# Norms between two blocks and the turning of x: a new order of passes in a 31-chunk kernel

## What is computed

```
u = rms_norm(x, norm_in_g)                 # x * rsqrt(mean(x*x) + 1e-6) * g
proj = u @ w_in                            # 1024 x 4096: pool_x, pool_z, m_x, m_z
y = concat(pool_mixer(pool_x) * silu(pool_z), mlstm_branch(m_x) * silu(m_z))
h = rms_norm(x + y @ w_out, norm_out_g)
x2 = layer_norm(h, ln_in_g_2, ln_in_b_2)
hh = x2 @ w_in_2                           # gMLP, convolution and window attention parts
out = layer_norm(ALPHA * x2 + concat(ya, yb, yc) @ w_out_2, post_ln_g_2, post_ln_b_2)
```

## Time and profile before

| | us |
|---|---|
| median of 3 runs (1269.55 to 1270.44) | 1270.35 |
| the profiled execution, whole | 1271.04 |
| its span on the core | 1269.2 |
| TensorE busy | 1214.5 |
| VectorE, GpSimd, ScalarE busy | 660.3, 466.2, 350.5 |
| mean granted TensorE clock, 1 being full | 0.986 |

### The profile page before, as it was taken

The page is one execution under the profiler, slowest core; times in us unless marked ns, Lnnn a source line. Parts: engine busy times, 40 slices in busy tenths (PEclk is TensorE's granted clock), DMA queues, the critical chain, the costliest instruction groups (busy, mean ns, idle before and its releaser), DMA issues.

```text
span 1269.2 us, 15967 instructions
## 1 busy us (share of the span) xinstructions
PE 1214.5 (96%) x5976; PEld 970.7 (76%) x5976; DVE 660.3 (52%) x1226; ACT 350.5 (28%) x710; POOL 466.2 (37%) x446
## 2 busy tenths in 40 slices
PE   4999999999999999999998998889999999999995
PEld 4778778788888878787786787768888886667784
DVE  6424274522366303167767924755696525445468
ACT  6211111100021212446565411231111143443311
POOL 1042242223454223444665644234242225443333
PEclk9999999999999999999999998999999999999998
DMA  6141121234312112200114411222111110051112
GB/s 213 43 141 42 34 74 34 100 133 132 74 34 67 59 67 89 83 23 25 55 39 141 175 34 67 83 96 67 51 36 64 59 34 34 2 191 34 34 51 116
DMA packets 72702, 92.84 MB, mean 73 GB/s; under 512 B 12721, under 2 KB 51849, under 8 KB 72114
## 3 DMA queue, kind: packets, MB, share of 16 engines
q1 hardware_dynamic: 63922, 87.62, 20.6%
q10 hardware_dynamic: 8704, 4.20, 1.2%
HBM read 74.45 MB, written 18.92 MB: 74 GB/s over the span
## 4 chain that ended last, share of the span: by engine, by line
PE 86%; DVE 6%; POOL 3%; issue 2%; ACT 1%; DMA 1%; SPq 1%; ACTq 0%; POOLq 0%; DVEq 0%
PE bank L821 21%; PE bank L823 20%; PE bank L822 20%; PE bank L1049 3%; PE bank L1066 3%; PE wide L1219 2%; PE wide L901 2%; PE bank L1200 2%; PE wide L1209 2%; PE wide L1059 2%; DVE res L1879 1%; PE bank L1009 1%; PE bank L1020 1%; POOL h L721 1%; PE bank L997 1%
## 5 line engine op out<-in xcount | busy, mean ns | idle before, releaser
L609 POOL CAST whi<-wraw 128x2048 fp32r<-128x2048 f32 x32 | 60.7, 1896 | 473.5 <-PE bank L823 371.7
L821 PE MATMUL bank<-u_hi,wlo 128*128 128x512 f32 x512 | 202.9, 396 | 4.0 <-DVE u_lo L1322 4.0
L822 PE MATMUL bank<-u_lo,whi 128*128 128x512 f32 x512 | 200.6, 392 | 0.0
L823 PE MATMUL bank<-u_hi,whi 128*128 128x512 f32 x512 | 200.5, 392 | 0.0
L611 POOL TENSOR_TENSOR wlo<-wraw,whi 128x2048 fp32r<-128x2048 f32 x33 | 156.2, 4735 | 8.0 <-ACT whi L2197 5.4
L821 PE MATMUL bank<-x_hi,wlo 128*128 128x512 f32 x320 | 128.7, 402 | 7.1 <-POOL wlo L611 4.6
L823 PE MATMUL bank<-x_hi,whi 128*128 128x512 f32 x320 | 125.4, 392 | 0.0
L822 PE MATMUL bank<-x_lo,whi 128*128 128x512 f32 x320 | 125.4, 392 | 0.0
L821 PEld LDWEIGHTS bank<-u_hi,wlo 128*128 128x128 f32 x512 | 96.9, 189 | 26.7 <-DVE u_lo L1322 4.5
L823 PEld LDWEIGHTS bank<-u_hi,whi 128*128 128x128 f32 x512 | 96.9, 189 | 20.6
L822 PEld LDWEIGHTS bank<-u_lo,whi 128*128 128x128 f32 x512 | 96.9, 189 | 20.5 <-issue 0.7
(11 more groups left out here) (318 smaller groups left out, 2416.4 us busy)
## 6 DMA issues: line engine op xcount, KB each, us to landing
wraw<-in_w_in SPq DMA_DIRECT2D x27, 1024.0 KB, 5.3
wraw<-in_w_out SPq DMA_DIRECT2D x12, 1024.0 KB, 5.1
xr<-in_x SPq DMA_DIRECT2D x8, 512.0 KB, 6.2
hst<-in_x SPq DMA_DIRECT2D x4, 1024.0 KB, 5.3
hpool<-hst SPq DMA_DIRECT2D x4, 1024.0 KB, 4.1
smz<-mzs SPq DMA_DIRECT2D x16, 256.0 KB, 2.0
wraw<-nmax ACTq DMA_DIRECT2D x32, 128.0 KB, 3.0
h<-hpool SPq DMA_DIRECT2D x4, 1024.0 KB, 6.7
```

The costliest lines, as they stand in the source:

```text
L609: g_.tensor_copy(whi[w % 2][:, :, :], wraw[:, :, :]).then_inc(s["w_hi"], 1)
L821: pe.matmul(ps, al, bh, start=(k == 0), stop=False)
L822: pe.matmul(ps, ah, bl, start=False, stop=False)
L823: return pe.matmul(ps, ah, bh, start=False, stop=(k == nk - 1))
```

## The change

**At the start.** SyncE loads x's tiles 4 to 7 right after weight chunk 0, ahead of the small gain vectors; `norm_in_g` is loaded by ScalarE's queue (`l_g`). ScalarE takes a root of ones first, so that its function table is loaded early, and takes each tile's root itself from the sum of squares (scale 1/D, bias `eps`); `var_x` is gone. TensorE waits for `norm_in_g` alone, turns it, and then turns each tile of x as it is scaled, into seven banks, with the eighth group of columns at the end. The rest of `VT` is turned after tile 3 of the product. VectorE no longer splits chunk 0; GpSimd does, in four parts (`g_part`), once four tiles are scaled, and starts chunk 1 only when all eight are. TensorE takes tile 0 of the product step by step as `u_lo` and the parts come; the second four tiles of x are turned in between the steps of tile 2.

**Between the blocks.** `norm_2` is cut in three: `tile_stats`, `tile_centre` and `tile_scale`. The scaling of tile t-1 follows the addition of tile t. GpSimd does seven of the left-half gains before it splits `W_OM + 3` (three before), and of the right half five (`GAINS`), after which `W_2` is split; VectorE does the last three. The first four groups of transposes follow step 12 of `PAIR`, and tile 0 of `W_BA` goes step by step.

```diff
-    LATE_2 = 6
+    LATE_2, GAINS = 6, 5
...
             wt(0)
-            rows = [("norm_in_g", 0), ("pool_scale", 0), ("conv_b", 0), ("mh_norm_w", 0), ("skip_w", 0)]
+            for t in range(4, NT):
+                sp_.dma_start(xr[:, t, :], x_v[:, t, :]).then_inc(l_x[t], 16)
+            rows = [("pool_scale", 0), ("conv_b", 0), ("mh_norm_w", 0), ("skip_w", 0)]
...
-            for t in range(4, NT):
-                sp_.dma_start(xr[:, t, :], x_v[:, t, :]).then_inc(l_x[t], 16)
...
+            g_.wait_ge(s["v_xn"], 4)
+            g_.wait_ge(s["w_hi"], 1)
+            for part in range(4):
+                ks = slice(2 * part, 2 * part + 2)
+                g_.tensor_tensor(wlo[0][:, ks, :], wraw[:, ks, :], whi[0][:, ks, :].bitcast(F32), ALU.subtract
+                                 ).then_inc(s["g_part" if part < 3 else "w_lo"], 1)
+            g_.wait_ge(s["v_xn"], NT)
             for w in range(1, W_MX + 2):
                 split(w)
...
             for t in range(NT):
                 gain(t, 0)
-                if t == 2:
+                if t == 6:
                     split(W_OM + 3)
-            for t in range(NT - 1):
+            for t in range(GAINS):
                 gain(t, 1)
-                if t == 4:
-                    split(W_2)
+            split(W_2)
             split(W_BB)
...
             pe.wait_ge(s["l_cst"], 16)
-            pe.wait_ge(s["l_rows"], 16 * 12)
-            ps = take(4, "v_vec", 1)
-            pe.transpose(ps[:, 0:V_CW2], vrow[:, :], cst[0:V_CW2, C_ID:C_ID + V_CW2])
-            pe.transpose(ps[:, V_CW2:V_N], vrow2[:, :], cst[0:V_N - V_CW2, C_ID:C_ID + V_N - V_CW2]
-                         ).then_inc(s["t_vec"], 1)
...
-            turn_x(0)
-            pe.wait_ge(s["v_ulo"], 8)
-            for i in range(2):
-                group(0, i, u_hi, u_lo, "a_px", i + 1)
-            turn_x(1)
-            pe.wait_ge(s["v_ulo"], 16)
+            pe.wait_ge(s["l_g"], 16)
+            ps = take(7, "v_vec", 1)
+            pe.transpose(ps[:, 0:8], vrow[0:8, :], cst[0:8, C_ID:C_ID + 8]).then_inc(s["t_vec"], 1)
+
+            for t in range(4):
+                pe.wait_ge(s["v_xn"], t + 1)
+                for j in range(KT - 1):
+                    ps = bank[j] if t else take(j, "v_ulo", j + 1)
+                    mm = pe.transpose(ps[:, t * P:(t + 1) * P], xr[:, t, j * P:(j + 1) * P], idn)
+                    if t == 3:
+                        mm.then_inc(s["t_x"], 1)
...
+            ps = ring_g("a_px", 1)
+            for k in range(KT):
+                if k < 6:
+                    pe.wait_ge(s["g_part"], k // 2 + 1)
+                else:
+                    pe.wait_ge(s["w_lo"], 1)
+                pe.wait_ge(s["v_ulo"], k + 1)
+                group(0, 0, u_hi, u_lo, "a_px", 1, ks=range(k, k + 1), ps=ps, whole=False)
+            group(0, 1, u_hi, u_lo, "a_px", 2)
+            pe.wait_ge(s["v_xn"], NT)
+            for j in range(3):
+                turn_x(j)
+            ps = ring_g("a_px", 3)
+            for k in range(KT):
+                pe.wait_ge(s["v_ulo"], KT + k + 1)
+                group(0, 2, u_hi, u_lo, "a_px", 3, ks=range(k, k + 1), ps=ps)
+                if k + 3 < KT:
+                    turn_x(k + 3)
...
-                for n in {13: (0, 1), 14: (2, 3, 4, 5), 15: (6, 7)}.get(i, ()):
+                for n in {12: (0, 1, 2, 3), 14: (4, 5), 15: (6, 7)}.get(i, ()):
                     turn_x2(n)
...
-            for t in range(5):
+            for t in range(4):
                 sum_h(3, t)
-                if t < 2:
-                    first_stats(NT - 2 + t)
-                norm_2(t)
+                if t:
+                    tile_scale(t - 1)
+                else:
+                    first_stats(NT - 2)
+                    first_stats(NT - 1)
+                tile_stats(t)
+                tile_centre(t)
+            tile_scale(3)
+            sum_h(3, 4)
             for n in range(4):
                 low_x2(n)
-            sum_h(3, 5)
+            tile_stats(4)
+            tile_centre(4)
             for n in range(4, 8):
                 low_x2(n)
+            sum_h(3, 5)
+            tile_scale(4)
             sum_h(3, 6)
             sum_h(3, 7)
             for t in range(5, NT):
-                norm_2(t)
+                tile_stats(t)
+                tile_centre(t)
+                if t > 5:
+                    tile_scale(t - 1)
+            tile_scale(NT - 1)
...
+            ac.wait_ge(s["g_init"], 2)
+            root(sd[:, 0:1], ones[:, 0:1])
+            ac.dma_start(vrow[0:8, :], I["norm_in_g"][0].rearrange("(j p) -> j p", p=P)).then_inc(s["l_g"], 16)
+            ac.wait_ge(s["a_sd"], 1)
...
             def root_x(t):
-                ac.wait_ge(s["v_var"], t + 1)
-                root(sd[:, t:t + 1], v1_[:, t:t + 1])
+                ac.wait_ge(s["a_ss"], t + 1)
+                ac.activation(sd[:, t:t + 1], ss[:, t:t + 1], ACT.Sqrt, scale=1.0 / D, bias=eps[:, 0:1]
+                              ).then_inc(s["a_sd"], 1)
...
-            for t in range(5):
+            for t in range(4):
                 square_h(t)
                 root_h(t)
-            high_x2(0, 1, 2, 3)
-
+            square_h(4)
             ac.wait_ge(s["l_wraw"], 16 * (W_2 + 1))
             ac.wait_ge(s["t_gemm"], done(W_2 - 2))
             ac.activation(whi[W_2 % 2][:, :, :], wraw[:, :, :], ACT.Copy).then_inc(s["w_hi"], 1)
-            high_x2(4, 5, 6, 7)
+            high_x2(*range(8))
+            root_h(4)
```

123 lines of the change are left out of this document (61 added, 62 removed), and 1 row of the table names.

## The result

| | before | after |
|---|---|---|
| median, us (lowest to highest) | 1269.95 (1269.37 to 1270.44) | 1249.51 (1248.26 to 1252.32) |
| profiled execution / its span | 1271.04 / 1269.2 | 1250.48 / 1248.6 |

A forecast was written before the change was run, and what follows sets the result against it. TensorE was taken as the bound, busy 1214.5 of 1269.2 us, so only its idle and slow stretches count. Gains of 10.9 (start) and 11.3 (between blocks), 22.2 us, gave 1248.8, or 1248.2 against the runs' median; range 1244.5 to 1253.0.

The forecast's parts named there:

- wait for `h` in the output product: TensorE's 3.93 us wait for a bank in the output product would go, bringing 6.8 us with the slow clock behind.
- The start: From weight chunk 0 to the bias table's matmul: first product at 15.5, matmul at 44.5 instead of 55.43, 10.9 us less.
- the 12.6: Time of the first product's tiles 0 and 1, kept from before: 10.88 us of work and 1.7 of slow clock.
- The first rival: At the start, `norm_in_g` lands as late as 14.5; first product at 19.4 at worst, 1251.7 us in all; chance 0.13.
- The rival of less granted clock: Over the whole span, TensorE rests less and the chip grants less clock; 1284 us at 3% less; chance 0.02.
- the tile of 5.2 us: Norm between the blocks: scaling, about 1.6 us, runs in VectorE's wait for square and gain; a tile falls from 6.8.
- the margin of 1.4 at the transposes: Between the blocks, the fourth scaling is over at about 793.3, and TensorE's transposes come at 794.7.
- TensorE sets the pace: In the norm's tiles VectorE needs 5.2 us, less than TensorE's 5.44; `W_BA`'s first product starts at 806.7, not 819.47.
- the sign to look for: In the changed profile, VectorE's right-half additions 5.44 us apart, each preceded by idle time that TensorE ends.
- what is late next: `W_BB`, loaded behind tile 4's store: TensorE idles 6.4 us and starts it at 824.0, not 835.27, 11.3 us less.
- The upper bound that I gave for this gain, 13.0: Most that `W_BB`'s start could gain: without the store's share and with the shorter subtraction of 4.58 us.
- The margin of 5 behind it: Behind `W_BB`, VectorE finishes the second four tiles at 831.4; they have until 836.6.

The follow-up runs named there:

- `middle_only`: The kernel before with only the part of the change between the blocks, the start as before; 1261.16 us, ratio 0.9915 to 0.9945.

## Why the prediction was right, and where it was off

| step | predicted | measured |
|---|---|---|
| first product | 15.5 | 16.09 |
| scaling of all tiles over | 27.1 at most | 25.54 |
| bias table's matmul | 44.5 (-10.9) | 44.99 (-10.44) |
| wait for `h` in the output product | none | none |
| a tile on VectorE | 5.2, TensorE's 5.44 decides | 5.88, VectorE decides |
| `W_BA` against before | -23.7 | -23.05 |
| wait for W_BB's low words | 6.4 | 6.41 |
| `W_BB` against before | -22.2 | -21.30 |

**The start** was right in each link: `whi` came 0.43 later, and what follows it until the first product took 1.62 instead of 1.46. Behind it tiles 0 and 1 took 12.59 (12.6 in the sum), tile 2 with its transposes 10.6 instead of 10.35, and the turned rest of the table 0.2 instead of 0.6. The slow stretch that I kept in the 12.6 is a matter of chance: in three kernels with this start it did not come, and the table stood at 43.1 to 43.5. That GpSimd's quarters would not hold `u_lo` is right (four in 2.73 us).

**The first rival** was false in after, and rightly named as the danger; its price was too low. I took the arrival of the old last vector, 14.5, as the worst; behind the loads of x that the change puts ahead it is 17.4, and costs 6.7 us in the profile and 7.2 to 8.6 in the medians instead of 3.5. The rival of less granted clock did not come either: the mean clock rose.

**The step that failed** is the tile of 5.2 us. I took the scaling's 1.6 off the old 6.8, as if it filled a wait that stayed as it was. The kernel that scales each tile at once, 6.79 a tile, shows the three things that this missed. On VectorE's way the reciprocal and the scaling took 1.40, not 1.6 (775.82 to 777.22). The scaling reads two tensors of SBUF, and so does the gain that GpSimd makes in that same time: the gain's record still begins 0.14 behind the square (767.12), but it grows from 1.29 to 1.64 and ends 1.16 after the scaling (767.60), so it had hardly got on beside it; that is 0.35. And L1668 stands until the gain is through, with L1669 still to come before the statistics: 0.14. 6.79 - 1.40 + 0.35 + 0.14 is the measured 5.88, 0.9 less and not 1.6. It cost almost nothing only because of the margin of 1.4 at the transposes, which is luck of the place and not of the reasoning: from the first of these additions to the fourth scaled tile VectorE took 24.7 (760.00 to 784.68) where the sum had 23.1, and 0.29 of waiting was left. So "TensorE sets the pace" was wrong and its result nearly right, and the sign to look for, additions 5.44 apart with TensorE's idle before them, did not show.

**`W_BB`** was right to a tenth: the load behind the store of tile 4, and the wait of 6.4. That I named it as what is late next is borne out by the load moved alone, which gave 4.9 us by the medians and 7.1 at its place. (The upper bound that I gave for this gain, 13.0, should have been 12.7: 0.6 for the store and 0.8 for the shorter subtraction. Nothing hangs on it.) The margin of 5 behind it was 5.9 (VectorE's last scaling ended at 821.3, TensorE came at 827.16), and it is this margin that the earlier load uses up. Of the 1.8 us by which the gain fell short, 0.46 were lost at the start and 0.44 between the blocks; 0.58 more behind `W_BB`, where the transposes followed after 13.19 us and not, as before, after 12.61, a slow stretch that I had taken over unchanged, and that took 12.3 to 13.8 in the kernels with the same code there; the rest is 0.1 to the end of the span and 0.2 between spans and medians.

## What to carry to other kernels

When an operation is moved into the time in which its engine waited for another, ask whether what is waited for can go on beside it: here a pass of 1.4 us, moved beside a gain that needed the same port, brought 0.9. The place of a load in its queue is worth all that waits behind it: one row of 4 KB was worth 6.7 to 8.6 us, one weight load moved ahead of one store 4.9 to 7.1. And take the clock's share out of two profiles before you explain a difference of 2 us between them: the same code lost 1.7 us to the clock near 420 in one execution and 5.1 in another.

## What the runs showed of the hardware

**The clock of the same code is not the same in each execution.** Between 415 and 430 us TensorE is busy without a break and yet loses the clock for a while; near 523 us it pauses in after (1.75 us) and in the kernel that scales each tile at once (2.01), in both for GpSimd's `Pm`. Windows of after:

```profile
415.00:430.00 15.00, 15.00 (x88) 13.73 (x88) 0.00 (x0) 3.07 (x6) 0.00 (x0) 0.89 0.07 24
524.00:532.00 8.00, 7.94 (x32) 5.93 (x33) 4.09 (x12) 3.05 (x8) 5.93 (x13) 1.00 0.11 31
```

and of the other, in which nothing of the program differs up to there:

```profile
415.00:430.00 15.00, 15.00 (x80) 13.98 (x80) 0.00 (x0) 2.55 (x6) 0.00 (x0) 0.77 0.05 19
524.00:532.00 8.00, 6.17 (x19) 4.54 (x20) 2.24 (x8) 2.46 (x6) 6.29 (x13) 0.79 0.12 32
```

Counting a window's length times what its clock lacks of 1, after lost 15 x 0.11 = 1.65 us in the first and nothing in the last; the other 15 x 0.23 = 3.45 and 8 x 0.21 = 1.68. The difference, 3.5 us, is what its addition at 763.50 stands behind after's 760.00. With `W_BB`'s load early the first window showed 0.68. The length of a pause does not decide alone: before the first product the clock stayed up after a pause of 2.39 us (with `W_BB`'s load early) and fell after one of 1.98 (after); with the old start the pause of 1.91 before the second half cost the clock in before (0.61 behind it) and not in `middle_only` (1.00). With the new start, where the clock stayed up, the bias table came at 43.1 to 43.5, else at 44.9 to 45.5. The Trainium skill, TensorE: Matmul & The Clock Gate, Part 1, says that the number of slow matmuls at the start of one and the same kernel varies from run to run; the runs agree, and show it in the middle of a kernel too.

**The shared port is held for one instruction at a time**, also against the smallest operation: the 128x1 addition took 0.15 us alone, 1.25 beside a gain and 3.37 beside a subtraction, and cutting the subtraction in four cut the hold from 3.47 to 1.40. The Trainium skill, SBUF — State Buffer, "Who interferes with whom", says that two SBUF inputs suffice for this contention and that the one that comes second stands for the whole instruction; the runs agree on both.

**The queue of a small load.** Issued from ScalarE's queue at 1.01 us (0.58 long), the row was there before 4.91, so within 3.9 us; in SyncE's queue, issued at 7.29 behind 5 MB of x and weights, it took 10.1 us from its issue. The Trainium skill, DMA: Bandwidth & Descriptors, "Issuing engines are not separate DMA queues", says that DMAs of all issuers run on the same 16 engines and that another issuer saves issuing time only; no run here shows whether another queue alone would help. Of the 12.5 us or more between the two arrivals 6.3 are the later issue, the rest a longer passage; whether the queue or the moment of issue makes it longer was not separated.
